# The low part of a weight chunk in eight GpSimd instructions of 128 columns

## The reference

```python
h = mixer_block(h, ...)   # norm; one wide projection; three kinds of attention (8 heads each); gates
h = conv_ffn(h, ...)      # norm; w_up; causal convolution of width 3; silu(gate) * val; w_down

proj = rms_norm(h, norm1_g) @ w_in
out_a = causal_block_attention(fq, fk, fv, log_decay)      # "FOX", with a decay
out_b = causal_block_attention(q, k, v_mla)                # "MLA", from low-rank latents, with rotation
out_c = sliding_window_attention(sq, sk, sv, sinks, slopes) # "SWA"
merged = sum over branches of sigmoid(gates) * (branch @ w_branch)
h = h + merged @ w_o
u = rms_norm(h, norm2_g) @ w_up
h = h + (silu(gate) * val) @ w_down
```

## Time and profile before

| what | us |
|---|---|
| median of three runs | 1999.71 |
| lowest and highest of them | 1999.29, 2000.68 |
| the profiled execution, whole | 1999.88 |
| its span, first to last instruction | 1998.1 |
| TensorE busy in the span | 1925.1 |
| VectorE busy | 1158.6 |
| GpSimd busy | 1024.3 |
| of that, the low parts of the chunks | 793.6 |
| ScalarE busy | 762.9 |

### The profile page before, as it was taken

The page is one execution under the profiler, slowest core; times in us unless marked ns, Lnnn a source line. Parts: engine busy times, 40 slices in busy tenths (PEclk is TensorE's granted clock), DMA queues, the critical chain, the costliest instruction groups (busy, mean ns, idle before and its releaser), DMA issues.

```text
span 1998.1 us, 36507 instructions
## 1 busy us (share of the span) xinstructions
PE 1925.1 (96%) x14436; PEld 1825.6 (91%) x14436; DVE 1158.6 (58%) x2125; ACT 762.9 (38%) x1463; POOL 1024.3 (51%) x1306
## 2 busy tenths in 40 slices
PE   6899999998999999999998999999999999999999
PEld 6889998888999999999997899988889999999887
DVE  7665476787464666652246654767865656566411
ACT  4555566555223222220035556666552232222100
POOL 7656554554354544455476565544534545545553
PEclk9999999999999999999999999999999999999999
DMA  4212111111132332223332121112112323332332
GB/s 148 73 45 65 54 60 48 54 54 53 56 127 85 96 96 85 86 94 96 95 107 75 43 65 55 62 45 64 44 53 64 129 86 95 96 96 87 104 95 95
DMA packets 44803, 156.32 MB, mean 78 GB/s; under 512 B 5012, under 2 KB 5268, under 8 KB 44504
## 3 DMA queue, kind: packets, MB, share of 16 engines
q1 hardware_dynamic: 44488, 153.75, 24.5%
q10 hardware_dynamic: 144, 0.22, 0.0%
HBM read 149.63 MB, written 4.26 MB: 77 GB/s over the span
## 4 chain that ended last, share of the span: by engine, by line
PE 78%; DVE 12%; ACT 4%; issue 3%; POOL 2%; DMA 0%; ACTq 0%; DVEq 0%; POOLq 0%
PE ps L1336 20%; PE ps L1339 20%; PE ps L1341 19%; PE ps L1567 5%; PE ps L1351 2%; PE ps L1347 2%; PE ps L1350 2%; PE ps L1355 2%; DVE rstd L1670 2%; PE ps L1480 1%; PE ps L1519 1%; DVE osum L1978 1%; DVE ps L1947 1%; PE ps L1525 1%; POOL wl L809 1%
## 5 line engine op out<-in xcount | busy, mean ns | idle before, releaser
L809 POOL TENSOR_TENSOR wl<-raw,wh 128x256 fp32r<-128x256 f32 x1076 | 793.6, 769 | 751.6 <-DVE wh L1649 743.8
L1336 PE MATMUL ps<-xh,wh 128*128 128x264 f32 (+1 forms) x2880 | 811.2, 303 | 21.7 <-DVE wl L1729 10.2
L1339 PE MATMUL ps<-xl,wh 128*128 128x264 f32 (+1 forms) x2880 | 764.0, 285 | 0.0
L1336 PEld LDWEIGHTS ps<-xh,wh 128*128 128x128 f32 x2880 | 546.9, 190 | 42.0 <-issue 27.0
L1341 PE MATMUL ps<-xh,wl 128*128 128x264 f32 (+1 forms) x2880 | 584.3, 284 | 0.0
L1339 PEld LDWEIGHTS ps<-xl,wh 128*128 128x128 f32 x2880 | 546.8, 190 | 17.1 <-issue 9.2
L1341 PEld LDWEIGHTS ps<-xh,wl 128*128 128x128 f32 x2880 | 450.8, 190 | 0.0
L1649 DVE CAST wh<-raw 128x1024 fp32r<-128x1024 f32 x270 | 201.9, 748 | 174.4 <-PE ps L1336 91.5
L1970 DVE TENSOR_TENSOR ps<-ps,cst 128x128 f32<-128x128 f32 (+6 forms) x240 | 75.1, 315 | 153.7 <-PE ps L1525 112.2
L1567 PE MATMUL ps<-pt,vx 128*128 128x512 f32 (+7 forms) x480 | 158.4, 411 | 2.7 <-ACT pt L1253 2.5
L1253 ACT ACTIVATE pt<-ps 128x256 f32<-128x256 f32 (+5 forms) x224 | 77.8, 363 | 102.5 <-DVE ps L1970 101.5
(11 more groups left out here) (194 smaller groups left out, 3413.6 us busy)
## 6 DMA issues: line engine op xcount, KB each, us to landing
raw<-weights SPq DMA_DIRECT2D x270, 512.0 KB, 3.5
h<-tokens SPq DMA_DIRECT2D x4, 528.0 KB, 6.7
h<-tokens SPq DMA_DIRECT2D x8, 264.0 KB, 4.8
residual<-h SPq DMA_DIRECT2D x8, 264.0 KB, 4.8
h<-residual SPq DMA_DIRECT2D x8, 264.0 KB, 5.2
out<-h SPq DMA_DIRECT2D x8, 256.0 KB, 4.6
cst<-constants SPq DMA_DIRECT2D x1, 1048.0 KB
extra<-positions SPq DMA_DIRECT2D x18, 4.1 KB
```

The costliest lines, as they stand in the source:

```text
L809: ins = nc.gpsimd.tensor_tensor(wl[c % SPLIT][:, part], raw[:, c % RAW, part], wh[c % SPLIT][:, part].bitcast(F32), ALU.subtract)
L1336: a = nc.tensor.matmul(out, a_hi, x_hi[:, sl], start=first, stop=False)
L1339: nc.tensor.matmul(out, a_hi, x_lo[:, sl], start=False, stop=False)
```

## The change

The width of a piece becomes a constant of its own, 128 columns, so that the low part of a chunk is made in eight instructions in place of four. Which columns are computed, from what, and which instruction signals (the last) stay as they were. Nothing else is edited.

```diff
 AHEAD = 2
+LOW_PIECE = P
 OT_RING = 6
...
                 pool.wait_ge(s_hi, c + 1)
                 settled()
-                for a in range(0, CW, CW // 4):
-                    part = slice(a, a + CW // 4)
+                for a in range(0, CW, LOW_PIECE):
+                    part = slice(a, a + LOW_PIECE)
                     ins = nc.gpsimd.tensor_tensor(wl[c % SPLIT][:, part], raw[:, c % RAW, part],
                                                   wh[c % SPLIT][:, part].bitcast(F32), ALU.subtract)
                 ins.then_inc(s_lo, 1)
```

## The result

The kernel with the finer pieces takes 2006.92 us, the median of seven runs (2004.49 to 2008.98), against 1999.71 before: ratio 1.0037, 95% interval 1.0027 to 1.0046. Of the seven executions of the kernel before, one took 3735.34 us and is left out of the ratio. The kernel is slower by 7.2 us (7.4 by the ratio) where +1.5 was forecast, and it lies above the range, which ended at 2006.0. The profiled execution took 2007.35 us, its span 2005.5, at the same mean granted clock of 0.992.

The account below looks back on a forecast made before the run. TensorE, busy 96% of the span, was taken to bound the kernel, with GpSimd setting start and seam. Terms 2.4 - 2.1 + 1.2 = +1.5 us on 1999.88 gave 2001.4, median 2001.2 us; range 1996.5 to 2006.0.

Parts of the forecast that it names:

- The price of the pieces: GpSimd's low part undisturbed: eight pieces take 3.42 us against 2.83 for four, 0.59 us more a chunk.
- Start and seam, +2.4: At the start and between the layers GpSimd alone sets the pace; four exposed low parts cost 0.59 us each.
- the number of its operations is fixed, and so is what they take from GpSimd before chunk 2: At the start, VectorE's intrusions cost GpSimd no more with eight pieces, so each low part adds only 0.59 us.
- the wait for merged: At the seam, TensorE's wait for this VectorE tile was to grow from 2.9 to about 4.1 us.
- Feed-forward, 0: In the feed-forward halves the longer low parts are hidden, with no wait of TensorE: 0 us.
- 3.0 us of room a chunk against 0.59: First feed-forward half: GpSimd idles 195.0 us over some 64 chunks, which covers the 0.59 us added to each.
- TensorE has other work meanwhile: Mixers, apart from the yq place: lateness of GpSimd's other low parts costs nothing; no size added.
- VectorE's gain, -2.1: Mixers: VectorE's waits behind shorter pieces halve, shortening two TensorE waits per mixer; 1.05 us back each, 2.1 for both.
- yq, +1.2: Mixers: two query pieces behind a chunk's low part come 0.59 us later, lengthening TensorE's wait near 115; 1.2 for both.
- The wait at 475: First mixer: TensorE's wait behind merged, square and rstd was to fall from 2.60 to 2.0 us.
- the rival in which GpSimd's other work comes late: Mixers: 0.59 us lost at six places per mixer, 7.1 us, +9.5 in all, 2009 us; chance 0.07.
- The size of the hold: Mixers: VectorE's 0.41 us wait for a GpSimd piece was to halve; the exclusive-lock reading gave 39% less.

Follow-up runs that it names:

- the ends alone: Eight pieces of 128 columns only in chunks 61 to 74 of each layer, four elsewhere, against the kernel before: 2003.36 us, ratio 1.0016.
- the once-more kernel: First 128 columns made twice, then four pieces of 256, at chunks 61 to 74 only, against the kernel before: 2000.06 us, ratio 1.0003.

## Why the prediction was wrong

**The price of the pieces: right.** 443 and 460 ns, 3.40 us for eight, against 0.443, 0.463 and 3.42. It is the price alone, and that was the trouble.

**Start and seam, +2.4: right in place, small in size.** Measured 3.0 (1.2 to 4.6) by the medians, 3.9 in the table by stretch. The step "the number of its operations is fixed, and so is what they take from GpSimd before chunk 2" held up to the low part of chunk 2: chunk 1's grew by 2.4 us, but VectorE was done sooner, the fills behind it took 1.8 us less, and the whole took 15.67 us in place of 15.09 (0.58 more, 0.59 said). It failed in the low part of chunk 2, which grew by 1.21 us and not 0.59, since a second of VectorE's operations got in where one had before. With 0.27 us by which this trace was late before any piece began, TensorE's chunk 2 came 2.06 us later where 1.2 was said. TensorE's wait there became 5.70 and not 6.3: TensorE had begun late on chunk 1 as well, after a wait of 1.70 us that the kernel before doesn't have. At the seam the wait for merged did not grow to 4.1; the lateness showed up as a wait for the low part (1.1 to 2.69) ahead of it.

**Feed-forward, 0: the step that failed.** "3.0 us of room a chunk against 0.59" is an average. In the 60 later chunks of each half it held (+0.02%, and no wait). But a wait in the feed-forward halves, which the prediction itself named as a sign of being wrong, came three times (0.70, 0.24 and 0.75 us). At the ends, two chunks follow each other closely and the room is far less: in the row at 649.07 the sixteen pieces of two chunks run on nearly without idle time between them (before, 0.84 us lay between the two), and the cast of the second chunk got in ahead of the last piece of the first. And around the product with w_o, of which the forecast said only that TensorE has other work meanwhile, VectorE's two-tile operations run all through the low parts. Eight pieces there took 5.27 us and not 3.76 + 0.59 = 4.35. In the first layer that cost TensorE nothing until the feed-forward chunks; in the second TensorE waited in the product itself (1.51 us at 1603). That these 14 chunks a layer cost 3.2 us is shown by the ends alone; that most of it is the doors and not the length, by the once-more kernel at the same chunks (1.0 us in its trace against 3.1).

**VectorE's gain, -2.1, and yq, +1.2: the second step that failed.** The hold halved more than said: 1.12 us became 0.85, a wait of 0.41 became 0.14. The wait at 475 shrank by 0.6 us, as said. But the one at 366 grew by 0.46 us. In the trace after, GpSimd's low part before it takes 5.24 us (3.27 before), and then yk begins at 365.04, just ahead of VectorE's q:

```profile
365.12 1.60 DVE L1895 TENSOR_TENSOR q<-krr,rstd 32x528 f32<-32x528 f32 x1
```

Before, q had come first and took 0.70 us. What was saved at the square and the rstd was lost there and more. And "elsewhere TensorE has other work meanwhile" failed for the copy of the extra rows, three waits, 4.2 us. The mixers were said to give back 0.9 us, and took 1.8: the rival in which GpSimd's other work comes late, at a quarter of its 7.1 us. The two missing terms, 3.2 at the ends and 2.7 in the mixers, with 0.6 at start and seam, make 6.5 us on top of +1.5; the measured difference to the forecast is 5.7.

**The size of the hold.** The forecast had the wait shrink in proportion to the piece: half of 0.41. It shrank by the whole streaming time of the columns taken away, 128 x 2.15 ns = 0.275 us: from 0.41 to 0.14. With 512 columns a wait was 1.66 - 0.71 = 0.95 us. All three fit "streaming time less 0.14 us" (0.55, 0.275 and 1.10 less 0.14); what the 0.14 consists of no run shows. The Trainium skill, SBUF — State Buffer, section "SBUF: two separate sides", has the pair's lock held for the whole instruction by the one who comes first. The rows agree but for a constant: VectorE's last 0.71 us begin 0.15 us before the end of the piece that kept it out, with 128, 256, 512 and 1024 columns alike (574.47 and 574.62 in the finer kernel, 474.14 and 474.29 in the one before, 472.12 and 472.27, 474.47 and 474.62), and 0.14 before the end of yk, which kept q out. So they don't show a lock that is given up early. What failed was the forecast's use of it, a wait that scales by 39% with the pieces' spacing; of a shorter piece such a wait saves the difference whole.

**Open.** One extra piece everywhere costs as much as eight short ones (+8.6 and +7.4 us), but not in the same places. By stretch, start and seam cost 4.2 us against 3.9, the ends 1.1 against 3.8, and the mixers 2.2 against -0.3. Two mixers that a kernel leaves alone lie between -3.3 and +0.5 us in six traces, the eight pieces (-0.3 and -0.2) among them, the piece made once more (2.2 and 3.0) above. So shorter pieces seem to give the mixers something back; one trace each and the medians' overlap leave it unproven. Why start and seam lose as much with five instructions as with eight no run tells.

## What to carry to other kernels

Price a longer step chunk by chunk where chunks come close together; the average room of a stage says nothing about its first and last. Where two engines contend, the number of cuts in one's work sets how often the other gets in: cut wide where the engine is in front, fine where the other is. And when the work of one engine grows, look at all that stands behind it in its queue, small copies included.

## What the runs showed of the hardware

An operation of VectorE on two SBUF tiles of 528 columns takes 0.71 us alone, 1.12 beside GpSimd pieces of 256 columns and 0.85 beside pieces of 128: the wait is some 0.14 us less than the piece's streaming time, at 512 columns too (0.95 us), and what is left of the operation begins 0.15 us before the piece ends. An operation that gets in ahead of a piece makes that piece 0.46 to 0.47 us longer (0.74 to 1.20, 0.46 to 0.93), and VectorE's cast of a chunk made one 0.50 us longer. A chunk of 1024 columns on GpSimd alone takes 3.40 us in eight instructions, 2.83 in four, 2.54 in two and 2.39 in one, so an instruction more costs 0.14 to 0.15 us.
